# A two-block float32 transformer kernel: PLE projections and block 0's gate products placed behind the last expert rows, their weight tiles requested at row 248 of 256

## What is computed

```python
x = x + merged @ w_out
x = x + peer_ffn(rmsnorm(x, norm_ffn), ...)
g_ple = sigmoid(rmsnorm(x, norm_ple) @ ple_gate)
x = x + g_ple * (p @ ple_proj)
# second block
h = rms_norm(x, g_mix) * (1 + scale) + shift
xin = h @ w_in_2  
```

## Time and profile before

| | us |
|---|---|
| median of 3 runs | 1464.54 |
| lowest, highest | 1463.68, 1467.13 |
| the profiled execution's own time | 1461.52 |
| its span, first to last instruction | 1459.6 |
| PE busy | 1282.1 (88%) |
| DVE busy | 723.5 (50%) |
| ACT busy | 260.1 (18%) |
| POOL busy | 319.1 (22%) |
| moved by DMA | 398.7 MB, 273 GB/s over the span |

### The profile page before, as it was taken

The page is one execution under the profiler, slowest core; times in us unless marked ns, Lnnn a source line. Parts: engine busy times, 40 slices in busy tenths (PEclk is TensorE's granted clock), DMA queues, the critical chain, the costliest instruction groups (busy, mean ns, idle before and its releaser), DMA issues.

```text
span 1459.6 us, 12490 instructions
## 1 busy us (share of the span) xinstructions
PE 1282.1 (88%) x4494; PEld 730.2 (50%) x4494; DVE 723.5 (50%) x1752; ACT 260.1 (18%) x628; POOL 319.1 (22%) x273
## 2 busy tenths in 40 slices
PE   6999998989888787778886896887899988999998
PEld 5757554575444343333332342333365466888743
DVE  2764632187665868785777845563244342010001
ACT  3132211121111111112211111122112422000000
POOL 0100000024443444544445434540000000000000
PEclk9999998999999999998999899999999999999999
DMA  7434565579999999998999979993334813433531
GB/s 261 168 139 173 173 242 205 180 279 374 383 421 406 422 418 420 421 421 359 418 421 421 421 309 421 423 421 120 115 125 173 300 54 114 173 129 130 201 124 50
DMA packets 98380, 398.73 MB, mean 273 GB/s; under 512 B 6352, under 2 KB 9808, under 8 KB 65424
## 3 DMA queue, kind: packets, MB, share of 16 engines
q0 software_dynamic: 37376, 270.29, 44.9%
q1 hardware_dynamic: 60944, 127.65, 24.5%
HBM read 396.86 MB, written 1.05 MB: 273 GB/s over the span
## 4 chain that ended last, share of the span: by engine, by line
PE 64%; DMA 16%; DVE 13%; ACT 3%; issue 3%; POOL 1%; DVEq 0%; SPq 0%; PEldq 0%; ACTq 0%
PE ps L490 18%; PE ps L502 14%; DMA big<-in_peer_uv,idx_t 14%; PE ps L742 13%; DVE big L1682 6%; PE ps L943 5%; PE ps L708 4%; PE ps L678 2%; DMA wring<-in_w_in 1%; PE ps L925 1%; PE ps L516 1%; PE ps L582 1%; POOL big L1282 1%; DMA wring<-in_w_up_hg 1%; ACT rows L1123 1%
## 5 line engine op out<-in xcount | busy, mean ns | idle before, releaser
L742 PE MATMUL ps<-big,rows 128*128 128x512 f32 x1024 | 490.0, 636 | 124.7 <-ACT rows L1123 124.5
L742 PEld LDWEIGHTS ps<-big,rows 128*128 128x128 f32 x1024 | 203.0, 203 | 405.1 <-issue 405.1
L1282 POOL DMA_INDIRECT big<-in_peer_uv,idx_t x256 | 306.4, 1197 | 422.5 <-PE ps L742 351.1
L1682 DVE CUSTOM_DVE_ANT_0 big<-big 128x1024 f32<-128x1024 f32 x256 | 305.9, 1224 | 120.0 <-DMA big<-in_peer_uv,idx_t 117.4
L490 PE MATMUL ps<-wring,big 128*128 128x512 f32 (+1 forms) x624 | 272.9, 594 | 11.8 <-DMA wring<-in_w_in 4.2
L502 PE MATMUL ps<-big,wring 128*128 128x256 f32 x960 | 209.5, 381 | 1.0 <-DVE big L1336 1.0
L502 PEld LDWEIGHTS ps<-big,wring 128*128 128x128 f32 x960 | 183.4, 191 | 27.0 <-issue 1.9
L490 PEld LDWEIGHTS ps<-wring,big 128*128 128x128 f32 x624 | 119.3, 194 | 153.3 <-issue 143.6
L1117 ACT ACTIVATE small<-small 128x4 f32<-128x4 f32 x64 | 13.0, 204 | 421.0 <-DVE small L1687 421.0
L1123 ACT ACTIVATE rows<-const,small 128x128 f32<-128x128 f32 x256 | 81.8, 390 | 19.2 <-DVE small L1691 18.9
L982 ACT ACTIVATE big<-ps 128x512 f32<-128x512 f32 x73 | 41.0, 595 | 240.1 <-PE ps L708 77.8
(11 more groups left out here) (234 smaller groups left out, 874.1 us busy)
## 6 DMA issues: line engine op xcount, KB each, us to landing
wring<-in_w_in SPq DMA_DIRECT2D x17, 2048.0 KB, 8.4
wring<-in_w_ada SPq DMA_DIRECT2D x12, 2048.0 KB, 8.3
wring<-in_w_gate SPq DMA_DIRECT2D x5, 2048.0 KB, 7.8
wring<-in_w_up SPq DMA_DIRECT2D x5, 2048.0 KB, 7.8
wring<-in_w_down SPq DMA_DIRECT2D x5, 2048.0 KB, 7.6
wring<-in_w_out SPq DMA_DIRECT2D x4, 2048.0 KB, 12.1
wring<-in_peer_wq SPq DMA_DIRECT2D x4, 2048.0 KB, 10.9
big<-in_peer_uv,idx_t POOLq DMA_INDIRECT x256, 12.3
```

The source lines that it names most:

```text
L742: last = nc.tensor.matmul(banks[h], diag[:, k % DIAGS, :], v_part[:, ring_at(k), h * 512:(h + 1) * 512], start=False, stop=(k % SLOTS == S ...
L1282: pool.indirect_dma_start(pair_ring[:, ring_at(k), :], None, a["peer_uv"], bass.IndirectOffsetOnAxis(idx_t[:, k:k + 1], 0))\
L1682: nc.vector.tensor_tensor_reduce(u_part[:, ring_at(k), :], u_part[:, ring_at(k), :], h_t[:, b, :], 1.0, 0.0, ALU.mult, ALU.add, a_dot[:, i ...
```

## The change

The four products of ple_proj, and ple0 and ple1 of block 0, leave the loop over the batches and stand behind the last one, ahead of block 0's "n4T". ACT's copies, tanh and `rms(3, 0)`, and DVE's `ple_add(0)`, move with them; ACT now copies block 1's x first and runs `rms(2, 1)` last. The turn of block 0 stays at m = 40, and DVE writes h3T at m = 42 in place of 48. SP waits ahead of the tile ple_proj until 62 x 4 = 248 rows are used, and all tiles behind it wait with it. The banks follow from the new order.

```diff
-PLE_PROJ, PLE_SCALE, PLE_TURN, PLE_GATE, PLE_ADD = 35, 40, 48, 56, 60
+PLE_SCALE = 40
...
-    p += half("experts", 0)
-    p += [("ple_proj", b, h) for b in range(NB) for h in range(2)]
-    p += half("n3T", 0) + [("ple0", 0), ("ple1", 0)] + half("experts", 1)
+    p += half("experts", 0) + half("n3T", 0) + half("experts", 1)
+    p += [("ple_proj", b, h) for b in range(NB) for h in range(2)] + [("ple0", 0), ("ple1", 0)]
...
+                if name == "ple_proj":
+                    sp.wait_ge(pair_free, (BATCHES - 2) * BATCH)
...
             for m in range(HALF_BATCHES, BATCHES):
-                if m == PLE_PROJ:
-                    pe.wait_ge(pT_landed, 16)
-                    by_rows("ple_proj", pT, k=2, w=512, wide=D)
                 if m == PLE_SCALE:
                     pe.wait_ge(h_ready, 5)
                     turn("n3T", h_t, [0])
-                if m == PLE_TURN:
-                    wait_turned("n3T", [0])
-                    by_rows("ple0", h3T, blocks=[0])
-                    by_rows("ple1", h3T, blocks=[0])
                 experts(m, banks)
...
+            pe.wait_ge(pT_landed, 16)
+            by_rows("ple_proj", pT, k=2, w=512, wide=D)
+            wait_turned("n3T", [0])
+            by_rows("ple0", h3T, blocks=[0])
+            by_rows("ple1", h3T, blocks=[0])
             pe.wait_ge(h_ready, 6)
             turn("n4T", h_t, [0])
...
             for m in range(HALF_BATCHES, BATCHES):
-                if m == PLE_PROJ:
-                    for b in range(NB):
-                        for h in range(2):
-                            move(pp[:, b, h * 512:(h + 1) * 512], "ple_proj", b, h)
-                if m == PLE_GATE:
-                    ple_tanh(0)
-                if m == PLE_ADD:
-                    act.wait_ge(x_whole, 3)
-                    rms(3, 0)
                 spread(m)
-            whole(1)
+            for h in range(2):
+                move(x[:, 1, h * 512:(h + 1) * 512], "experts", 1, h)
+            for b in range(NB):
+                for h in range(2):
+                    move(pp[:, b, h * 512:(h + 1) * 512], "ple_proj", b, h)
+            for h in range(2):
+                wait_moved(act, "experts", 1, h)
+            ple_tanh(0)
+            act.wait_ge(x_whole, 3)
+            rms(3, 0)
+            rms(2, 1)
             ple_tanh(1)
...
-                if m == PLE_TURN:
+                if m == PLE_SCALE + 2:
                     turned("n3T", 0, h3T, lane[:, L_PLE:L_PLE + KD])
-                if m == PLE_ADD:
-                    ple_add(0)
                 dots(m)
...
+            for h in range(2):
+                for b in range(NB):
+                    wait_moved(dve, "ple_proj", b, h)
+            ple_add(0)
             scale(3, 0)
```

## The result

| | before | after |
|---|---|---|
| median, us | 1465.61 (4 runs) | 1480.26 (4 runs) |
| lowest to highest | 1463.68 to 1467.13 | 1478.86 to 1488.48 |
| profiled execution | 1461.52, span 1459.6 | 1480.17, span 1478.5 |

The ratio is 1.0112, 95% interval 1.0073 to 1.0152: 16.4 us slower, where 9.6 were forecast. The sign was right, the size was not.

What follows compares the result with a forecast made beforehand. The expert stage was taken as bound by DMA bytes. Loads -11.9, hole -9.8, end +2.5 and path +28.8 us sum to +9.6: 1471.1 us for a run like the profiled one, 1474 as a median, range 1466 to 1481.

Steps and rivals of the forecast that it cites:

- The bound of the stage: Expert stage: bound by DMA bytes, 2.49 us for a row, with some slack on PE.
- the path behind it: From the experts' last matmul to in2_q's first product: 32.8 us against 3.97, so 28.8 us more.
- ple0 at nearly nothing: ple0's tile load in the expert stage: it used a hole in the rows, costing 0.5 us, between 0 and 5.0.
- in2_q at 5.0 us: in2_q's tile load in the expert stage: 2.10 MB with no hole, displacing 5.0 us of rows.
- ple_proj at 2.5 us: ple_proj's tile load in the expert stage: 1.05 MB with no hole, displacing 2.5 us of rows.
- ple1 at 3.9: ple1's tile load in the expert stage: partly filling a gap, costing 3.9 us, between 3.6 and 5.0.
- The hole at 9.8 us: Behind block 0's two gate products in the stage: 9.8 us of lost transfer given back, bounds 8 and 10.
- The end at 2.5 us: Last expert rows: three tiles loading beside them delay the experts' end by 2.5 us, bounds 0 and 12.4.
- Sum: Whole kernel: stage 21.7 us shorter, end 2.5 and path 28.8 us longer, together 9.6 us slower.
- every byte counts: Rival on the stage's loads: all tile bytes displace rows, 17.4 us given back, total +4.1 us; 17%.
- Equal turns at the end: Rival on the last rows: three tiles ahead take 7.5 us, or a tile is late, total +14.6 us; 10%.
- PE's time was not regained: Judges the rival that the stage regains all 20.6 us of PE products plus 17.4 of bytes, total -6.7 us; 6%.

Runs made afterwards that it cites:

- e5: The kernel before with only in2_q's tile load held until 248 rows are used; ratio 0.9990, 1.5 us faster, interval holding zero.
- e9: The changed kernel run again, its wait only written in another way; ratio 1.0115 to the kernel before, 16.8 us slower.
- e4: The changed kernel with ple_proj's tile, products and copies back in the expert stage; ratio 1.0050 to the kernel before, 7.3 us slower.
- e6: The kernel before with only ple1's tile load held until row 128 is used; ratio 1.0007, no gain.
- e2: The changed kernel with SP's tile loads held until all 256 rows are used; ratio 1.0145 to the kernel before, 21.2 us slower.
- e7: The kernel before with all three PLE tiles held until 144 rows are used, ple_proj's products at batch 39 instead of 35; ratio 1.0078, 11.4 us slower.
- e8: The kernel before with gate products at batches 48 and 51, ple1 held until row 128, in2_q until 248 rows; ratio 0.9956, 6.4 us faster.
- e3: The kernel before with block 0's two gate products split, ple0 at batch 48, ple1 at batch 51; ratio 0.9960, 5.9 us faster.
- e1: The changed kernel without SP's wait for 248 rows, so the three tiles load in block 0's half; ratio 1.0135 to the kernel before, 19.7 us slower.
- e10: The kernel before with block 0's gate products one batch apart, ple0 at batch 48, ple1 at 49; ratio 0.9999.

## Why the prediction was right or wrong

- **The bound of the stage, and the path behind it.** Right. 28.8 us forecast, 28.75 measured, each of its pieces to 0.4 us, the slow turn among them (1.97 us, granted clock 0.50).
- **ple0 at nearly nothing, in2_q at 5.0 us.** Right. ple0 and ple_proj together cost 0.9 us. For in2_q the ledger has 4.9 from row 139 to 167 (4.1 to 5.5 in the other runs in which it does not load there, but 2.9 in e5).
- **ple_proj at 2.5 us and ple1 at 3.9.** Here the first step failed: "It displaces 2.5 us", since the total was full while ple_proj loaded. A full DMA during a load does not say that it stays full without it. ple_proj and ple0 together cost 0.9 us, not 3.0. The three loads gave back 3.7 and 4.6 us (row 35 to 139 in after and e9), not 6.9; over all executions their price is about 5. ple1's price was right at row 91, where after is 4.1 us early, but 1.8 of it was gone four rows later (1.0 to 1.4 in e9, e4 and e6, nothing in e2, e7 and e8), for a reason that is not shown.
- **The hole at 9.8 us.** The second mis-sized term. It is right as lost transfer and its cause is shown by e3; in rows it is 7.9 us, and 5 to 7 in three other kernels of the same placement.
- **The end at 2.5 us.** The third. It measured 5.4: the last row came 3.4 us later and the last batch took 2.0 us more, part of it at half clock, for which the forecast had no term. That 2.5 is what the rows lost beside e1 and e2 is luck: it took 3.15 MB of rows with 0.8 MB of tiles ahead of the last, and it was 1.82 and 2.80 MB.
- **Sum.** Stage 3.7 + 4.9 + 7.9 and 0.5 in small changes = 17.0, for 21.7; end 5.4, for 2.5; path 28.75: +17.2 from row 35 to in2_q in the profile of after, and 15.7 in e9. The measured 16.4 lies between. So the loss is found to within what the executions differ. The reference made part of it hard to see: the profiled execution of before was early by 2.4 us at row 35 and had a larger hole than its likes.
- **The rivals.** That every byte counts is refuted for block 0's half and true behind it (e7). Equal turns at the end: more bytes went ahead of the last row than that rival took from the rows' share, 2.80 MB of tiles beside 1.82 of rows, yet the last row came 3.4 us late where it feared 7.5. PE's time was not regained: e4 shows it free in the stage.
- **Not settled.** Why e10 has no gain in time, beyond its slow last batch; the price of the three loads to better than 1 or 2 us; how much of the slow last batch belongs to the loads; and why row 254 is late with nothing loading.

## What to carry to other kernels

In this stage bound by bytes, PE work was free as long as one piece was shorter than what the ring of buffers covers. If a piece is longer, split it, with some batches between the parts, before you think of taking it out: the split made this kernel 5.9 us faster, while moving that work, ple_proj's and their tiles behind the stage cost 16. A load beside a stream costs its bytes only where the stream would be without holes; look at what the stream does just behind each load before you count it. Beside the last transfers of a stream a load costs less than where the stream is full (3.4 us in rows for these 5.2 MB, against 13.7 in e7), but count what a late last piece does to the work that waits for it: here the last batch took 2 us longer behind a longer idle time.

## What the runs showed of the hardware

The share of two queues is not fixed: a tile got 0.22 of the rows' bytes while some five rows were outstanding, and 2.4 times their bytes (1.11 to 0.47 MB) while the last ones were running out. From SP's request to the first tile bytes 3 us passed (974.04 to 977). And executions of kernels that are alike up to row 35 differ by up to 4.3 us there, about a quarter of the effect under study; most of that arises ahead of the change's first part, so a comparison of two profiles needs a ledger that starts at the change.
